# A fused encoder layer: the first norm's weight spread by a matmul, convolution blocks in column halves, and later weight blocks subtracted on VectorE

## The reference

```python
h = rms_norm(x, mix_norm)                       # x: 256 tokens x 1024
proj = h @ w_in                                 # -> u | v | z | xBC | dt | gate_a | gate_b
y_a = sgu_branch(u, v)                          # gelu, layer norm of v, 128x128 mixing per head
y_b = mamba2_branch(z, xBC, dt)                 # conv of 4 taps, chunked scan, gated group norm
merged = sigmoid(gate_a) * (y_a @ w_a) + sigmoid(gate_b) * (y_b @ w_b)
x = x + merged @ w_out
x = x + moe_ffn(rms_norm(x, ffn_norm))          # top 4 of 32 experts, w1 1024x2048, w2 1024x1024
x = x + sigmoid(rms_norm(x) @ w_ple_gate) * (p @ w_ple_proj)
return rms_norm(x, final_norm)
```

## Time and profile before

| what | value |
|---|---|
| median of 3 runs | 1301.29 us (1300.56 to 1303.34) |
| the profiled execution, its own time | 1297.66 us |
| its span, first to last instruction | 1295.9 us |
| mean granted TensorE clock | 0.987 |
| PE busy | 94% |
| DVE, ACT, POOL busy | 27%, 16%, 15% |
| DMA | 457.69 MB, 353 GB/s over the span |

### The profile page before, as it was taken

How to read it: one execution, slowest core, us unless ns; L and a number is a source line. 1 busy time by engine, 2 the same in 40 slices (tenths; PEclk the granted TensorE clock), 3 DMA queues, 4 the chain that set the end, 5 groups by cost and what they waited for, 6 DMA issues and landing times.

```text
span 1295.9 us, 15355 instructions
## 1 busy us (share of the span) xinstructions
PE 1223.8 (94%) x6299; PEld 646.4 (50%) x6299; DVE 351.1 (27%) x668; ACT 202.0 (16%) x263; POOL 193.4 (15%) x57
## 2 busy tenths in 40 slices
PE   5998999989999999999999999999999999999976
PEld 5986888866444444444433333334433333333432
DVE  3528650443122121112211211112211121111222
ACT  4654545342000000000000000000000000000011
POOL 6855548860000000000000000000000000000000
PEclk9988999999999999999999999999999999999989
DMA  8543357858899999999999999999999999999900
GB/s 271 193 133 128 126 187 275 302 181 345 373 428 429 429 428 428 429 428 429 428 429 429 428 428 428 428 428 428 429 428 429 428 429 427 428 429 429 428 13 32
DMA packets 61879, 457.69 MB, mean 353 GB/s; under 512 B 7320, under 2 KB 16896, under 8 KB 37280
## 3 DMA queue, kind: packets, MB, share of 16 engines
q1 hardware_dynamic: 61856, 457.36, 86.0%
HBM read 456.29 MB, written 1.05 MB: 353 GB/s over the span
## 4 chain that ended last, share of the span: by engine, by line
DMA 48%; PE 48%; DVE 1%; ACT 1%; issue 1%; SPq 0%; POOL 0%; DVEq 0%; ACTq 0%
DMA wring<-in_w_dram 47%; PE bank L854 15%; PE bank L601 6%; PE bank L603 6%; PE bank L602 6%; PE bank L899 4%; PE bank L831 2%; PE bank L973 2%; PE bank L840 1%; PE bank L588 1%; PE bank L707 1%; PE bank L729 1%; DMA z<-in_mix_norm_dram 0%; PE bank L862 0%; DMA blk<-in_w_in_dram 0%
## 5 line engine op out<-in xcount | busy, mean ns | idle before, releaser
L854 PE MATMUL bank<-wring,hT 128*64 128x512 f32 x2048 | 453.9, 596 | 30.1 <-DMA wring<-in_w_dram 29.3
L854 PEld LDWEIGHTS bank<-wring,hT 128*64 128x64 f32 x2048 | 139.8, 137 | 321.4 <-issue 252.1
L899 PE MATMUL bank<-wring,xbcT 128*64 128x512 f32 x1024 | 228.5, 599 | 0.0
L554 POOL TENSOR_TENSOR blk_lo<-blk,blk_hi 128x2048 fp32r<-128x2048 f32 (+1 forms) x41 | 186.3, 4556 | 86.8 <-ACT blk_hi L991 74.7
L899 PEld LDWEIGHTS bank<-wring,xbcT 128*64 128x64 f32 x1024 | 71.1, 137 | 153.4 <-issue 153.4
L1545 DVE TENSOR_SCALAR xbcT<-bank 128x512 f32<-128x512 f32 x32 | 22.1, 692 | 448.7 <-PE bank L862 448.7
L831 PEld LDWEIGHTS bank<-xbcT,ga 128*128 128x128 f32 x1056 | 122.9, 192 | 4.0 <-DVE xbcT L1509 1.2
L831 PE MATMUL bank<-xbcT,ga 128*128 128x64 f32 x1056 | 121.6, 273 | 0.9 <-DVE xbcT L1509 0.9
L1166 ACT ACTIVATE xbcT<-xbcT 128x512 f32<-128x512 f32 x32 | 20.2, 631 | 522.8 <-DVE xbcT L1545 522.8
L991 ACT ACTIVATE blk_hi<-blk 128x2048 fp32r<-128x2048 f32 x39 | 74.5, 1915 | 112.1 <-DMA blk<-in_w_in_dram 70.6
L1559 DVE COPY xbcT<-bank 128x256 f32<-128x256 f32 x32 | 13.6, 424 | 274.1 <-PE bank L904 274.1
(11 more groups left out here) (238 smaller groups left out, 910.6 us busy)
## 6 DMA issues: line engine op xcount, KB each, us to landing
wring<-in_w_dram SPq DMA_DIRECT2D x192, 2048.0 KB, 22.0
blk<-in_w_in_dram SPq DMA_DIRECT2D x28, 1024.0 KB, 5.2
blk<-in_w_branch_a_dram SPq DMA_DIRECT2D x4, 1024.0 KB, 5.4
blk<-in_w_branch_b_dram SPq DMA_DIRECT2D x4, 1024.0 KB, 6.5
blk<-in_w_out_dram SPq DMA_DIRECT2D x4, 1024.0 KB, 5.0
blk<-in_w_ple_gate_dram SPq DMA_DIRECT2D x4, 1024.0 KB, 9.0
x<-in_x_dram SPq DMA_DIRECT2D x4, 512.0 KB, 5.1
v<-in_w_ple_proj_dram SPq DMA_DIRECT2D x1, 1024.0 KB, 8.8
```

The lines of the kernel that those rows point to most:

```text
L554: nc.gpsimd.tensor_tensor(dst, raw, hi.bitcast(FP32), ALU.subtract).then_inc(done, 1)
L854: last = mm(bank[dh * SLOTS:(dh + 1) * SLOTS, :], xgT[:, k, :], wring[:, 2 * c + kk, off + dh * W:off + (dh + 1) * W], start=(k == 0), sto ...
L899: last = mm(YB[dh * SLOTS:(dh + 1) * SLOTS, :], actT[:, kk * P + c * SLOTS:kk * P + (c + 1) * SLOTS], wring[:, at, (kk % 2) * D + dh * W:( ...
```

## The change

Four edits.

1. `mix_norm` is loaded as one row (4 KB) and ahead of x. Two PE matmuls with a row of ones spread it over the partitions into PSUM banks 6 and 7. DVE's scaling reads it from there, in four pieces of 512 columns, and PE starts the transposes of a piece when it is there. ACT squares both halves of the tokens.
2. ACT rounds the first column half of block 0 before it rounds the transposed activations. All eight blocks of xBC are rounded by ACT and subtracted by POOL in column halves.
3. PE makes the products of an xBC column half in three passes of 8 matmuls: high x high, low x high, high x low. The first pass waits for the rounding alone, the second for POOL, the third for `a_lo`.
4. POOL subtracts only blocks 0 to 7. Blocks 8 to 39 are subtracted by DVE (`weight_low`), at places written into DVE's order: block 8 and 9 in the convolution's loop, 10 after it, 11 and 12 before the first statistics of v, 13 before the second, 14 after them, 15 before v is normalised, 16 and 17 after it, 18 after `cb`, 19 after `mix`, and so on. DVE takes `sguw` and `acs` before the second statistics of v.

The diff, cut to its core; what stands behind a `#` is a remark of this text:

```diff
-            load(mix_gain, vec(mix_norm), mix_loaded)      # SP; now the row, ahead of x
+            load(mix_row, mix_norm, mix_loaded)
...
+            for i in range(XBC_HALVES):                    # POOL, which then is done with blocks
+                for c in range(2):
+                    pool.wait_ge(blk_high, rounded(i, c))
+                    subtract(column_half(blk_lo[:, i % NB, :], c), column_half(blk[:, i % NB, :], c),
+                             column_half(high(i), c), xbc_low)
...
+            pe.wait_ge(mix_loaded, 16)                     # PE
+            for h in range(HALVES):
+                last = mm(banks[6 + h][:, :], ones[0:1, :], mix_row[:, h * W:(h + 1) * W], start=True, stop=True)
+            last.then_inc(gain_spread, 1)
+            for t in range(TT):
                 for h in range(2):
+                    pe.wait_ge(xn_done, 2 * t + h + 1)
                     transposes(("xT", t, h), [v[:, t, (4 * h + i) * P:(4 * h + i + 1) * P] for i in range(4)])
-            wait_taken(pe, *all_of("xT"))
+            pe.wait_ge(act_high, 4)
...
+                        pe.wait_ge(blk_high, rounded(i, c))
                         for k in range(KT):
+                            mm(to, col(high(i), k), a_hi[:, k, :], start=(k == 0), stop=False)
+                        pe.wait_ge(xbc_low, 2 * i + c + 1)
+                        for k in range(KT):
+                            mm(to, col(raw_lo, k), a_hi[:, k, :], start=False, stop=False)
+                        if i == 0 and c == 0:
+                            wait_taken(pe, *all_of("xT"))
+                        for k in range(KT):
+                            last = mm(to, col(high(i), k), a_lo[:, k, :], start=False, stop=(k == KT - 1))
...
+            for t in range(TT):                            # ACT
+                act.wait_ge(x_loaded[t], 16)
+                fn(u[:, t, :], x[:, t, :], ACT.Square, accum_out=ssq[:, t:t + 1]).then_inc(ssq_done, 1)
...
+            split(0, [0])
+            act.wait_ge(xn_done, 2 * TT)
             high_parts("xT", a_hi)
-            split(0)
+            split(0, [1])
...
+            def weight_low(*halves):                       # DVE
+                for i in halves:
+                    dve.wait_ge(blk_high, rounded(i))
+                    tt(blk_lo[:, i % NB, :], blk[:, i % NB, :], high(i).bitcast(FP32), ALU.subtract).then_inc(nat_low, 1)
...
+            dve.wait_ge(gain_spread, 1)
+            for t in range(TT):
+                for h in range(HALVES):
+                    cols = slice(h * W, (h + 1) * W)
+                    stt(v[:, t, cols], x[:, t, cols], rstd[:, t:t + 1], banks[6 + h][:, :], ALU.mult,
+                        ALU.mult).then_inc(xn_done, 1)
...
+                if i >= 6:                                 # in the convolution's loop
+                    weight_low(i + 2)
             conv_silu(*order[-1], len(order) - 1)
+            weight_low(10)
...
             for b in range(HALVES):
+                if b:
+                    take_small()                           # sguw and acs, moved here from below
+                weight_low(*([11, 12] if b == 0 else [13]))
...
+            weight_low(14)                                 # after the statistics
+            weight_low(15)                                 # before v is normalised
+            weight_low(16, 17)                             # after v_done
+            weight_low(18)                                 # after cb
+            weight_low(19)                                 # after mix, before seg
+                    weight_low(*([20] if b == 0 else [21, 22]))   # before z's b=0 and b=1
+            weight_low(23, 24)                             # after the scan's sums
+            weight_low(25, 26)                             # before low_parts("yaT")
+            weight_low(27, 28, 29, 30)                     # after it
+            weight_low(31, 32)                             # before gate_a(0) and low_parts("ybT")
+            weight_low(33, 34)                             # after them
+                    weight_low(35 + 2 * b, 36 + 2 * b)     # before wb's b=0 and b=1
+            weight_low(39)                                 # before low_parts("mT")
```

More of the change, by code:

```diff
@@ L398, in weights_used, with rounded, column_half @@
                 wait_filled(eng, (kind, b, 1))
+        def rounded(i, c=1):
+            return 2 * i + c + 1 if i < XBC_HALVES else XBC_HALVES + i + 1
+        def column_half(ap, c):
+            return per_k(ap)[:, :, c * P:(c + 1) * P]
         def high(i):
@@ L981, in _, with split @@
             fn = nc.scalar.activation
-            def split(i):
+            def split(i, parts=range(2)):
                 act.wait_ge(blk_loaded[i % NB], 16 * (i // NB + 1))
[L986 to L989, removed]
+                if i < XBC_HALVES:
+                    for c in parts:
+                        fn(column_half(high(i), c), column_half(blk[:, i % NB, :], c), ACT.Copy).then_inc(blk_high, 1)
                 else:
@@ L1292, in _, with take_small @@
             cp(dtx[:, 5], dtx[:, 0]).then_inc(empty(("dt",)), 1)
+            def take_small():
+                link(nc.vector.memset(sgu_wT[CHUNK:P, :, 0:CHUNK], 0.0))
+                for h in range(2):
+                    name = ("sguw", h)
+                    wait_filled(dve, name)
+                    cp(sgu_wT[0:CHUNK, 4 * h:4 * h + 4, :], seg4(bank_of(name)[0:CHUNK, :]))
+                    cp(sgu_wT[CHUNK:P, 4 * h:4 * h + 4, CHUNK:P], seg4(bank_of(name)[CHUNK:P, :])[:, :, CHUNK:P]).then_inc(empty(name), 1)
+                name = ("acs",)
+                wait_filled(dve, name)
+                both = bank_of(name)[:, 0:TT * 2 * HEADS].rearrange("p (c a h) -> p c a h", c=TT, a=2)
+                link(cp(acs[:, :, 0, :], both[:, :, 0, :]))
+                tt(acs[:, :, 1, :], both[:, :, 1, :], acs[:, :, 0, :], ALU.subtract).then_inc(acs_done, 1)
+                dve.wait_ge(acs_done, 1)
+                cp(dtx[:, 5], dtx[:, 0]).then_inc(empty(name), 1)
             for b in range(HALVES):
+                if b:
+                    take_small()
+                weight_low(*([11, 12] if b == 0 else [13]))
                 for t in range(TT):
@@ L1304, in _ @@
             nc.vector.reciprocal(ssq[:], ssq[:]).then_inc(v_var, 1)
-            link(nc.vector.memset(sgu_wT[CHUNK:P, :, 0:CHUNK], 0.0))
-            for h in range(2):
-                name = ("sguw", h)
-                wait_filled(dve, name)
-                cp(sgu_wT[0:CHUNK, 4 * h:4 * h + 4, :], seg4(bank_of(name)[0:CHUNK, :]))
-                cp(sgu_wT[CHUNK:P, 4 * h:4 * h + 4, CHUNK:P], seg4(bank_of(name)[CHUNK:P, :])[:, :, CHUNK:P]).then_inc(empty(name), 1)
-            name = ("acs",)
-            wait_filled(dve, name)
-            both = bank_of(name)[:, 0:TT * 2 * HEADS].rearrange("p (c a h) -> p c a h", c=TT, a=2)
-            link(cp(acs[:, :, 0, :], both[:, :, 0, :]))
-            tt(acs[:, :, 1, :], both[:, :, 1, :], acs[:, :, 0, :], ALU.subtract).then_inc(acs_done, 1)
-            dve.wait_ge(acs_done, 1)
-            cp(dtx[:, 5], dtx[:, 0]).then_inc(empty(name), 1)
+            weight_low(14)
             def heads(ap):
```

35 lines of the change are left out of this document (10 added, 25 removed).

## The result

| | before | after |
|---|---|---|
| median of 12 runs each, taken in turn | 1302.49 us (1294.21 to 1304.13) | 1293.02 us (1288.83 to 1297.42) |
| ratio, 95% interval | | 0.9935 [0.9917, 0.9953] |
| profiled execution, its own time; span | 1297.66; 1295.9 | 1293.22; 1291.5 |
| mean granted clock of that execution | 0.987 | 0.985 |

Faster by 0.65%, 9.5 us by the medians and 4.4 us between the two profiled executions. At an equal clock of 0.985 to 0.987 before takes 1297 to 1300 us and after 1289 to 1294: about 7 us, where the prediction summed 6.5. How far the mean clock is given to a kernel from outside, and how far the kernel's own waits make it, is open; so the 7 us is an estimate.

The account below looks back on a forecast made before the run. The prediction took expert weight transfers and, in the front stage, PE with three holes as the bound. It summed 4.3 + 4.0 - 1.0 - 0.8 = 6.5 us gained, giving 1294.8 us, range 1290.8 to 1299.5.

Parts of the forecast that it names:

- the likeliest case: Whole kernel: 6.5 us gained, 1294.8 us, own range 1293.3 to 1296.8; chance 0.50 for gains of 4.5 to 8.
- all goes better: Rival: clock rises early at the start (1.6) and stays up ahead of z (1.0); gain 9, 1292.2 us; chance 0.16.
- The start: Up to PE's first xBC product: it comes at 12.8 instead of 17.12, 4.3 us gained.
- The hole ahead of u: PE's 5.77 us wait for DVE to take `sguw` goes, with the lower clock behind it: 7.7 us taken alone.
- DVE's row of work up to z: DVE's queue from 96.0 sums to 41.4 us, so PE waits 3.7 ahead of z; 4.0 of 7.7 us gained.
- The clock behind the hole: At z, after the new 3.7 us wait: PE's clock may fall, 1.0 us lost, bounds 0 and 2.0.
- z to wo: Behind z's start: block 32 covered by about 1 us; only block 39 delays `b_lo` ahead of wo, 0.8 us lost.
- The path to the end: Expert stage: its first request follows PE's use of the first expert's first chunk, so front-stage gains move the end equally.
- The lock-out: DVE two-input and POOL SBUF instructions exclude each other; blocks 8 to 10 could each lose up to 2.4 us, sum unchanged.
- the start alone pays: Rival: DVE's queue is longer than summed and the clock falls; gain about 3, 1298.3 us; chance 0.18.
- DVE becomes the bound: Rival: seven subtractions ahead of z make it slower; gains used up at 3.2 us a block; chance 0.09.
- the gain does not reach the end: Rival: the experts' last-requested first chunks, not PE, open the expert stage and eat the gain; 1301 us; chance 0.07.

Follow-up runs that it names:

- double_13_to_19: Kernel after, with one more two-input DVE instruction of 2048 columns ahead of each of blocks 13 to 19, result thrown away: 1310.39 us, ratio 1.0075.
- dve_late_small: Kernel after, with DVE taking `sguw` and `acs` behind v's statistics as before: 1294.42 us, ratio 0.9951.
- start_alone: Kernel before with edits 1 to 3 only; POOL subtracts every block and DVE's order is as before: 1289.61 us, ratio 0.9916.
- pool_after_v: Kernel after, but POOL subtracts every block and begins block 16 only when v is normalised: 1286.76 us, ratio 0.9888.
- dve_8_to_17: Kernel after, but DVE subtracts only blocks 8 to 17 and POOL those from 18 on: 1286.24 us, ratio 0.9895.
- start_order_pool: Kernel after, with POOL subtracting every block (edits 1 to 3 and the moved `sguw` and `acs`): 1303.82 us, ratio 1.0024.
- row_alone: Kernel before with the first edit alone (row loaded and spread by PE, DVE in four pieces, squares on ACT): 1297.20 us, ratio 0.9988.

## Why the prediction was right, and where it was not

The time fell by 0.65%; forecast 1294.8 us from a median of 1301.29 (0.5%), measured 1293.02 from 1302.49. That lies inside the stated range of 1290.8 to 1299.5, but not in the likeliest case's own, 1293.3 to 1296.8: a gain of 8.3 from the forecast's median, or 9.5 from the measured one, is the size of the case *all goes better*. What came in the trace is the likeliest case: at wo's start the lead is 6.4 us where 6.5 was summed. That the two are so near is partly luck. The start gave 3.3 at v's end and not 4.3, DVE's row of work let z gain 5.5 and not 4.0, and the clock behind the hole took 1.6 and not 1.0; the three errors cancel. Step by step:

- **The start, 4.3 us forecast**: 3.1 in the profiled execution, 4.0 to 4.3 in the five other kernels with all three edits and block 0 in one load (first product at 12.8 to 13.1), and 3.2 in `double_13_to_19`. The difference is the term of block 0's load. The text put it at 9, and said that a landing at 10.8 would end the roundings near 14: it landed at 10.92 and they ended at 13.93. The working of the 9 was loose: the rate slices sum to 2.6 MB at 9.7, not at 10.3, and they hold bytes of block 1 too, which had been requested by then. In the five others block 0 held ACT until 9.1 to 10.1. PE began to transpose at 8.38 (8.45 forecast). What the text calls seven halves, 24.47 to 64.89, are the seven blocks 1 to 7. The spreading matmuls, a cost without a row, took 3.78 us from 2.75 on and were hidden, as assumed. In four of those five the products ran at the upper level from the first one (8 in 1.21 us, where the kernel after took 2.08), which is the 0 to 1.6 us that the text kept in its range: their v ends at 89.5 to 89.8 and not at 92.02. At the first product the row has 0.7 of this gain and the passes 2.7, by the two runs that have one each; at v's end only the passes' part is left.
- **The hole ahead of u**: gone, 9.28 at u against 3.27 at v's end, 6.0 us. The text laid it to DVE's order alone; 2.3 of it were POOL's lock on L1303, as `dve_late_small` against `start_alone` shows.
- **DVE's row of work up to z**: 39.8 us (92.72 to 132.5) where 41.4 was summed. A subtraction costs 2.29, as the slope of two rows gave; neighbours overlap by some 0.1 each, which a sum of durations overstates. So the new wait was 2.2 and not 3.7. PE itself was ready at 130.4, 34.5 after u's start. `double_13_to_19` shows that this row of work is the bound, us for us. The remark that DVE would ask for block 19 at 135.1 was a slip: by the text's own sum it is about 132.9, and 135.2 is its end. Nothing hung on it.
- **The clock behind the hole**: eight products at 0.43 instead of 0.228, 1.6 us lost; 1.0 was taken, in bounds of 0 to 2. The Trainium skill (TensorE: Matmul & The Clock Gate, What's actually happening) says that the point at which the clock changes depends on a count that runs free of the kernel, and so varies from run to run. The runs here are in line with it: the mean clock of the kernel before went from 0.978 to 0.990 over its runs, and the wait ahead of wo was followed by the lower level in the kernel after and by the upper one in `dve_late_small`, which differs little (last section).
- **z to wo**: no new wait of PE up to wb's end, 7.2 us kept all the way. **wo**: 0.8 lost forecast, 0.8 lost (7.19 to 6.37).
- **Not in the sum**: the lower clock level behind the hole ahead of wo, 1.6 us, where the text had gone by before's short holes that cost nothing, and 2.1 and 2.4 around the first expert, of which 1.7 came back there. The last part gave 2.6 back. One execution of each kernel is traced, so it isn't shown which of these would come again.
- **The path to the end**: the text hung the end on the request for the second expert's first chunk. In the traces SP issues it at 315.40 after and 315.65 before, 0.2 apart, while the later experts led by 1.8 to 2.0. So what PE does in the first expert behind this request still moved the end.
- **The lock-out**: the text was right that blocks 8 to 10 would not meet POOL (its last xBC half ended at 54.8, DVE's first block began at 61.49), but it stopped there. What it missed is that a quiet POOL is what makes the move of `sguw` and `acs` pay at all. The Trainium skill (SBUF — State Buffer, Who interferes with whom) lists more than DVE's two-input instructions: copies and `tensor_scalar` in the modes that use both port pairs lock with GpSimd too. The traces agree: a copy at 3.01 instead of 0.18, two `TENSOR_SCALAR` at 9.99 instead of 1.53, both only beside POOL, while copies out of PSUM kept their 0.68 and 0.43.
- **The rivals**: *the start alone pays* fell inside the kernel (u and z lead by more than v), yet `start_alone` is as fast at the end, so there it is not refuted; *all goes better* came in other kernels (`pool_after_v`, `dve_8_to_17`), whose starts had the upper level and whose z had no wait; *DVE becomes the bound* needed 3.2 us a block and had 2.29; *the gain does not reach the end* fell for the mechanism that it named, the last chunks: 4.4 us were there in the profiled execution, 9.5 by the medians.

What stays open is how much of the 4.4 to 9.5 us belongs to the kernel and how much to the clock that its runs were granted. The comparison at equal clocks, about 7 us, is the best that these runs give, and whether a kernel's holes themselves set that clock was not tried.

## What to carry to other kernels

Move work from POOL to DVE by counting what the whole row of DVE's instructions has to finish before PE's next need, and stop where it is full: here ten blocks left PE without a wait ahead of z, and with twelve it waited 2.2 us. Before a step is moved earlier, ask what the other engines will then start earlier: u sooner drew POOL's subtractions onto DVE's work, and the move alone cost 0.7%. Where one wait keeps two engines that share a port apart, it can be worth more than moving the work: 17 us here, against 10.8 for the subtractions moved to DVE, both from `start_order_pool`.

## What the runs showed of the hardware that was not expected

- **One kernel's time follows the granted clock of the run.** The kernel before took 1293.9 to 1295.6 us at a mean clock of 0.989 to 0.990, 1297.4 to 1300.4 at 0.986, 1302.3 to 1303.5 at 0.983 and 1306.1 to 1308.1 at 0.978, some 1.1 us for each 0.001. An effect of 5 us is read from runs of equal clock, or from many.
- **A POOL subtraction of 4.6 us holds a DVE instruction of some kinds for its whole rest, however small that one is**: a copy of 32 columns took 3.0 to 3.2 us in three kernels, a `TENSOR_SCALAR` of two columns 2.48 in before, and one instruction after the other is caught when POOL has a new block each time. The statistics of v (1.29) and copies out of PSUM were not held beside the same subtraction.
- **A hole may or may not cost the clock.** Behind nearly the same wait ahead of wo, 2.79 and 2.69 us, PE's timelines show 0.43 for a product in the kernel after:
```profile
269.98 0.63 PE L606 MATMUL bank<-blk_hi,b_hi 128*128 128x512 f32 x1
270.40 0.63 PE L607 MATMUL bank<-blk_lo,b_hi 128*128 128x512 f32 x1
```
and 0.23 in `dve_late_small`:
```profile
269.23 0.47 PE L605 MATMUL bank<-blk_hi,b_lo 128*128 128x512 f32 x1 [2.69 <-DVE b_lo L1245]
269.54 0.40 PE L606 MATMUL bank<-blk_hi,b_hi 128*128 128x512 f32 x1
269.77 0.39 PE L607 MATMUL bank<-blk_lo,b_hi 128*128 128x512 f32 x1
```
In the seven kernels with waits of 1.29 to 1.83 us at this place, and in before, the upper level held. In `row_alone`, with 2.10, it fell three products later, from 277.45 to 280.83, and in `double_13_to_19`, with 2.98, at once.
